# Interleaved token blocks and product streams from the last column to the first in a decoder layer, with two gaps of 128 bytes

## What is computed

```
h = rms_norm(x, attn_norm_g);  proj = h @ w_in                      # 2048 x 13312
kv = rms_norm(mem, mem_norm_g) @ w_mem_kv                           # 2048 x 2048
merged = (sigmoid(g_da) * (o_da @ w_o_da) + sigmoid(g_ret) * (o_ret @ w_o_ret)
          + sigmoid(g_mem) * (o_mem @ w_o_mem))
x = x + merged @ w_out
hf = rms_norm(x, ffn_norm_g)
x = x + (silu(hf @ w_ffn_gate) * (hf @ w_ffn_up)) @ w_ffn_down      # width 5632
```

## Time and profile before

| | us |
|---|---|
| median of 2 runs | 1623.02 (1622.66 to 1623.38) |
| span of the profiled execution | 1620.8 |
| PE busy | 1613.9 |
| DVE busy | 1305.7 |
| ACT busy | 915.7 |
| POOL busy | 80.6 |

### The profile page before, as it was taken

The page is one execution under the profiler, slowest core; times in us unless marked ns, Lnnn a source line. Parts: engine busy times, 40 slices in busy tenths (PEclk is TensorE's granted clock), DMA queues, the critical chain, the costliest instruction groups (busy, mean ns, idle before and its releaser), DMA issues.

```text
span 1620.8 us, 19825 instructions
## 1 busy us (share of the span) xinstructions
PE 1613.9 (100%) x7355; PEld 1336.1 (82%) x7355; DVE 1305.7 (81%) x1361; ACT 915.7 (56%) x993; POOL 80.6 (5%) x73
## 2 busy tenths in 40 slices
PE   9999999999999999999999999999999999999999
PEld 7888888888888888888888888888888888888887
DVE  5565658898677777787975589999999999999995
ACT  6654555555555544444554455665656655656653
POOL 0000000000011000000000000100100100100101
PEclk9999999999999999999999999999999999999999
DMA  9776555666645555566666746868868868868866
GB/s 351 268 214 194 157 150 177 213 201 196 193 156 168 165 162 172 180 186 202 206 233 192 258 147 210 256 211 254 243 216 245 252 206 251 246 217 240 251 213 177
DMA packets 178013, 341.45 MB, mean 211 GB/s; under 512 B 11792, under 2 KB 16400, under 8 KB 177168
## 3 DMA queue, kind: packets, MB, share of 16 engines
q1 hardware_dynamic: 167056, 319.45, 60.8%
q0 software_dynamic: 10880, 20.97, 7.1%
HBM read 317.31 MB, written 2.10 MB: 197 GB/s over the span
## 4 chain that ended last, share of the span: by engine, by line
PE 85%; issue 11%; DVE 1%; POOL 1%; DMA 1%; ACT 0%; DVEq 0%; ACTq 0%; SPq 0%; POOLq 0%
PE acc L1600 38%; PE at L1692 9%; PE at L1691 9%; PE at L1690 9%; PE acc L1692 5%; PE acc L1690 5%; PE acc L1691 5%; PE at L1600 3%; PE at L1622 2%; POOL rstd L487 1%; PE at L1653 0%; PE at L1670 0%; DMA raw<-in_w_mem_kv 0%; DMA raw<-in_w_in 0%; DVE w_lo L938 0%
## 5 line engine op out<-in xcount | busy, mean ns | idle before, releaser
L938 DVE TENSOR_TENSOR w_lo<-raw,w_hi 128x1024 fp32r<-128x1024 f32 x313 | 378.9, 1223 | 196.0 <-ACT w_hi L514 190.7
L514 ACT ACTIVATE w_hi<-raw 128x1024 fp32r<-128x1024 f32 x313 | 330.6, 1060 | 341.9 <-PE acc L1600 274.0
L1600 PE MATMUL acc<-w_hi,hT_hi 128*128 128x512 f32 x664 | 262.8, 396 | 0.0
L1600 PE MATMUL acc<-w_hi,hT_lo 128*128 128x512 f32 x664 | 258.8, 390 | 0.0
L1600 PE MATMUL acc<-w_lo,hT_hi 128*128 128x512 f32 x664 | 258.6, 390 | 0.0
L866 ACT ACTIVATE f_hi<-sum 128x2048 fp32r<-128x2048 f32 x60 | 115.3, 1922 | 122.0 <-DVE sum L1479 118.8
L1600 PE MATMUL acc<-w_hi,oT_hi 128*128 128x512 f32 x384 | 151.2, 394 | 1.1 <-DVE oT_lo L964 1.1
L1600 PE MATMUL acc<-w_hi,oT_lo 128*128 128x512 f32 x384 | 149.7, 390 | 0.0
L1600 PE MATMUL acc<-w_lo,oT_hi 128*128 128x512 f32 x384 | 149.4, 389 | 0.0
L1445 DVE TENSOR_TENSOR f_raw_rest<-f_raw,f_hi 128x2048 fp32r<-128x2048 f32 x64 | 145.3, 2284 | 4.3 <-ACT f_hi L856 4.3
L1600 PEld LDWEIGHTS acc<-w_hi,hT_hi 128*128 128x128 f32 x664 | 124.7, 188 | 27.4 <-issue 1.3
(11 more groups left out here) (348 smaller groups left out, 2858.6 us busy)
## 6 DMA issues: line engine op xcount, KB each, us to landing
raw<-in_w_in SPq DMA_DIRECT2D x208, 512.0 KB, 3.8
f_raw<-in_w_ffn_down SPq DMA_DIRECT2D x88, 512.0 KB, 5.0
f_raw<-in_w_ffn_gate SPq DMA_DIRECT2D x80, 512.0 KB, 4.0
f_raw<-in_w_ffn_up SPq DMA_DIRECT2D x80, 512.0 KB, 5.2
proj<-down POOLq DMA_DIRECT2D x40, 512.0 KB, 6.5
raw<-in_w_mem_kv SPq DMA_DIRECT2D x32, 512.0 KB, 5.7
raw<-in_w_out SPq DMA_DIRECT2D x32, 512.0 KB, 3.9
raw<-in_w_o_mem SPq DMA_DIRECT2D x16, 512.0 KB, 5.0
```

Of the source, the lines that this page charges most:

```text
L514: act.activation(w_hi[:, s % RING], raw[:, s % RING], ACT.Copy).then_inc(hi_done, 1)
L938: v.tensor_tensor(w_lo[:, s % RING], raw[:, s % RING], w_hi[:, s % RING].bitcast(F32), ALU.subtract).then_inc(lo_done, 1)
L1600: e = pe.matmul(dst, a[:, k0 + k, tok], w[:, s % RING, k, :], start=first and k == 0 and n == 0, stop=last and k == 1 and n == 2)
```

## The change

Three things, with the same number of instructions on each engine.

- The tokens of the two blocks are interleaved in `hT`, `aT` and the `cmb` tiles: token block `t` is now every second word (`t::TB`), and the four combinations lie as two interleaved pairs. The transposes that fill `hT` and `aT` write every second word of PSUM, and the host lays out the transposed input in that order. `oT` stays as it was.
- Each product of 512 columns streams its moving operand from the last column to the first, and writes its output in that order too, so that the result is the same.
- A tile of 32 unused words (128 bytes) stands behind `hT_hi` and another behind `hT_lo`.

```diff
@@ -135,7 +135,9 @@
         sb("align", [P, ALIGN])
         hT_hi = sb("hT_hi", [P, KD, TOK], F32R)
+        sb("gap_hi", [P, 32])
         hT_lo = sb("hT_lo", [P, KD, TOK], F32R)
+        sb("gap_lo", [P, 32])
...
-            ("rows_t1", rows_tile, F32), ("sum1", quad_tile, F32), ("cmb_hi", [P, 4, 4, P], F32R),
+            ("rows_t1", rows_tile, F32), ("sum1", quad_tile, F32), ("cmb_hi", [P, 4, 2, P, 2], F32R),
...
@@ -1426,17 +1428,16 @@
-                a11, a12 = pairs[:, :, 0, 0:P], pairs[:, :, 1, 0:P]
-                a21, a22 = pairs[:, :, 0, P:2 * P], pairs[:, :, 1, P:2 * P]
-                v.tensor_tensor(mixed[:, :, 3], a11, a21, ALU.subtract).then_inc(done, 1)
-                step(v.tensor_tensor(mixed[:, :, 0], a22, a21, ALU.subtract), done, 3)
...
+                a11, a12, a21, a22 = (pairs[:, :, k, t::TB] for t in range(TB) for k in range(2))
+                v.tensor_tensor(mixed[:, :, 1, :, 1], a11, a21, ALU.subtract).then_inc(done, 1)
+                step(v.tensor_tensor(mixed[:, :, 0, :, 0], a22, a21, ALU.subtract), done, 3)
...
             def three_passes(s, hi, lo, k0, p, k, t, first, last):
-                tok = slice(t * P, (t + 1) * P)
+                tok = slice(t, TOK, TB) if hi is hT_hi else slice(t * P, (t + 1) * P)
                 dst = acc[p][:, t, :] if p < 2 else at[:, 2 * p - 4 + t, :]
                 for n, (a, w) in enumerate(((hi, w_hi), (hi, w_lo), (lo, w_hi))):
-                    e = pe.matmul(dst, a[:, k0 + k, tok], w[:, s % RING, k, :],
+                    e = pe.matmul(dst[:, ::-1], a[:, k0 + k, tok], w[:, s % RING, k, ::-1],
                                   start=first and k == 0 and n == 0, stop=last and k == 1 and n == 2)
...
-                        e = turn(at[:, k % 4, t * P:(t + 1) * P], src[:, t, c0 + k * P:c0 + (k + 1) * P])
+                        e = turn(at[:, k % 4, t:TOK:TB], src[:, t, c0 + k * P:c0 + (k + 1) * P])
...
             def product(dst, hi, lo, whi, wlo, first, last):
 
+                dst, whi, wlo = dst[:, ::-1], whi[:, ::-1], wlo[:, ::-1]
                 pe.matmul(dst, hi, whi, start=first, stop=False)
...
             def block_a(t, k):
-                return hT_hi[:, k, t * P:(t + 1) * P], hT_lo[:, k, t * P:(t + 1) * P]
+                return hT_hi[:, k, t::TB], hT_lo[:, k, t::TB]
...
             def turn_acts(dst):
                 for k in range(4):
                     for t in range(TB):
-                        c0 = (k % 2) * 256 + t * P
-                        e = turn(dst[:, k // 2, c0:c0 + P], gt[:, t, k * P:(k + 1) * P])
+                        c0 = (k % 2) * TOK
+                        e = turn(dst[:, k // 2, c0 + t:c0 + TOK:TB], gt[:, t, k * P:(k + 1) * P])
...
             def combined(i, c):
-                return cmb_hi[:, i, c, :] if i < 4 else cmb_hi4[:, i - 4, c, :], cmb_lo[:, i, c, :]
+                hi = cmb_hi[:, i] if i < 4 else cmb_hi4[:, i - 4]
+                return hi[:, c // 2, :, c % 2], cmb_lo[:, i, c // 2, :, c % 2]
...
-        "x_t": inputs["x"][0].T, "mem_t": inputs["mem"][0].T,
+        "x_t": inputs["x"][0].T.reshape(D, TB, P).transpose(0, 2, 1).reshape(D, TOK), "mem_t": inputs["mem"][0].T,
```

More of the change, by code:

```diff
@@ L163, in program @@
                     for t in range(TB):
-                        for name, shape, dt in (("r_cmb", [P, 4, 4, P], F32R), ("r_sum", [P, 4, NCOL], F32R if stage else F32),
+                        for name, shape, dt in (("r_cmb", [P, 4, 2, P, 2], F32R), ("r_sum", [P, 4, NCOL], F32R if stage else F32),
                                                 ("r_hi", [P, 4, NCOL], F32R), ("r_act", [P, 2 * NCOL], F32)):
@@ L168, in program @@
                 for name, shape, dt in (("r_rows", [P, 4, 4, P], F32), ("r_whole", [P, 2, TOK], F32),
-                                        ("r_mixed", [P, 4, P], F32)):
+                                        ("r_mixed", [P, 2, P, 2], F32)):
                     branch[0, name, 0] = overlay.enter_context(nc.sbuf_tensor(name, shape, dt))
@@ L834, in _ @@
                     act.wait_ge(cmb_f, 5)
-                    act.activation(cmb_hi[:], sums[1][:].rearrange("p q (c m) -> p q c m", c=4),
+                    act.activation(cmb_hi[:], sums[1][:].rearrange("p q (a m b) -> p q a m b", a=2, b=2),
                                    ACT.Copy).then_inc(cmb_split, 1)
@@ L838, in _ @@
                     act.wait_ge(cmb_f4, 5)
-                    act.activation(cmb_hi4[:], sums[0][:, 2:4].rearrange("p q (c m) -> p q c m", c=4),
+                    act.activation(cmb_hi4[:], sums[0][:, 2:4].rearrange("p q (a m b) -> p q a m b", a=2, b=2),
                                    ACT.Copy).then_inc(cmb_split, 1)
@@ L1069, in memory_attention @@
                 if i is not None:
[L1070 to L1073, removed]
+                    a11, a12, a21, a22 = (p_whole[:, k, t::TB] for t in range(TB) for k in range(2))
+                    v.tensor_tensor(p_mixed[:, 1, :, 1], a11, a21, ALU.subtract).then_inc(p_cmb, 1)
+                    step(v.tensor_tensor(p_mixed[:, 0, :, 0], a22, a21, ALU.subtract), p_cmb, i * 5 + 3)
+                    step(v.scalar_tensor_tensor(out=p_mixed[:, 0, :, 1], in0=p_mixed[:, 0, :, 0], scalar=-1.0, in1=a11,
                                                 op0=ALU.mult, op1=ALU.subtract), p_cmb, i * 5 + 4)
-                    v.tensor_tensor(p_mixed[:, 2], a12, p_mixed[:, 1], ALU.add).then_inc(p_cmb, 1)
+                    v.tensor_tensor(p_mixed[:, 1, :, 0], a12, p_mixed[:, 0, :, 1], ALU.add).then_inc(p_cmb, 1)
                 i = head_slot(x, 6)
@@ L1315, in _ @@
                     if s == 2:
[L1316 to L1319, removed]
+                        a11, a12, a21, a22 = (r_whole[:, k, t::TB] for t in range(TB) for k in range(2))
+                        v.tensor_tensor(r_mixed[:, 1, :, 1], a11, a21, ALU.subtract).then_inc(r_cmb, 1)
+                        step(v.tensor_tensor(r_mixed[:, 0, :, 0], a22, a21, ALU.subtract), r_cmb, i * 5 + 3)
+                        step(v.scalar_tensor_tensor(out=r_mixed[:, 0, :, 1], in0=r_mixed[:, 0, :, 0], scalar=-1.0, in1=a11,
                                                     op0=ALU.mult, op1=ALU.subtract), r_cmb, i * 5 + 4)
-                        v.tensor_tensor(r_mixed[:, 2], a12, r_mixed[:, 1], ALU.add).then_inc(r_cmb, 1)
+                        v.tensor_tensor(r_mixed[:, 1, :, 0], a12, r_mixed[:, 0, :, 1], ALU.add).then_inc(r_cmb, 1)
                     if s == 6:
@@ L1428, in combine @@
                                      hT_lo[:, 2 * q0:2 * q1, :].bitcast(F32), ALU.add), done, 1)
-                a11, a12 = pairs[:, :, 0, 0:P], pairs[:, :, 1, 0:P]
-                a21, a22 = pairs[:, :, 0, P:2 * P], pairs[:, :, 1, P:2 * P]
-                v.tensor_tensor(mixed[:, :, 3], a11, a21, ALU.subtract).then_inc(done, 1)
-                step(v.tensor_tensor(mixed[:, :, 0], a22, a21, ALU.subtract), done, 3)
-                step(v.scalar_tensor_tensor(out=mixed[:, :, 1], in0=mixed[:, :, 0], scalar=-1.0, in1=a11, op0=ALU.mult,
+                a11, a12, a21, a22 = (pairs[:, :, k, t::TB] for t in range(TB) for k in range(2))
+                v.tensor_tensor(mixed[:, :, 1, :, 1], a11, a21, ALU.subtract).then_inc(done, 1)
+                step(v.tensor_tensor(mixed[:, :, 0, :, 0], a22, a21, ALU.subtract), done, 3)
+                step(v.scalar_tensor_tensor(out=mixed[:, :, 0, :, 1], in0=mixed[:, :, 0, :, 0], scalar=-1.0, in1=a11, op0=ALU.mult,
                                             op1=ALU.subtract), done, 4)
-                step(v.tensor_tensor(mixed[:, :, 2], a12, mixed[:, :, 1], ALU.add), done, 5)
-            mixed4 = sums[1][:].rearrange("p q (c m) -> p q c m", c=4)
+                step(v.tensor_tensor(mixed[:, :, 1, :, 0], a12, mixed[:, :, 0, :, 1], ALU.add), done, 5)
+            mixed4 = sums[1][:].rearrange("p q (a m b) -> p q a m b", a=2, b=2)
             last = sums[0][:, 0:2].rearrange("p q (k c) -> p q k c", k=2)
-            mixed1 = sums[0][:, 2:4].rearrange("p q (c m) -> p q c m", c=4)
+            mixed1 = sums[0][:, 2:4].rearrange("p q (a m b) -> p q a m b", a=2, b=2)
             def low_whole(f, p, u):
@@ L1717, in combined @@
                 def combined(c):
-                    return p_cmb_hi[:, i, c, :], p_cmb_lo[:, i, c, :]
+                    return p_cmb_hi[:, i, c // 2, :, c % 2], p_cmb_lo[:, i, c // 2, :, c % 2]
                 pe.wait_ge(lo_done, g + 2)
@@ L1847, in combined @@
                 def combined(c):
-                    return r_cmb_hi[:, i, c, :], r_cmb_lo[:, i, c, :]
+                    return r_cmb_hi[:, i, c // 2, :, c % 2], r_cmb_lo[:, i, c // 2, :, c % 2]
                 pe.wait_ge(lo_done, g + 2)
@@ L1960, in down_half @@
                 for k in range(4):
-                    e = product(at[:, 2 * (n % 2) + t, :], hi[:, k, t * P:(t + 1) * P],
-                                lo[:, k, t * P:(t + 1) * P], *whole(f, p, u, k), k == 0, k == 3)
```

(2 more changed lines are left out.)

8 lines of the change are left out of this document (4 added, 4 removed).

## The result

The changed kernel takes 1663.78 us (two runs, 1663.71 and 1663.84) against 1623.02: slower by the ratio 1.0251, 95% interval 1.0207 to 1.0295. The forecast was 1561 us, faster, with a range of 1550 to 1638; the time lies above it. The profiled execution's span is 1661.9 us, 41.1 more than before.

The account below looks back on a forecast made before the run. TensorE's start-to-start interval, 6771 x 0.2268 us, was taken to bound 95% of the span. Gains of 30.8 (products without oT), 7.6 (oT) and 24.1 us (feed-forward loop) sum to 62.5, giving 1561 us, range 1550 to 1638.

Parts of the forecast that it names:

- The excess: 512-column products start each 0.2268 us, 11.3 ns over the 0.2155 of plain float32 rows; 76.5 us over 6771 products.
- the loop's second bound: Feed-forward loop: VectorE's chain, 59.7 us a round, outlasts TensorE's 59.1, so the loop gives 24.1 us and not 30.5.
- the sum: Whole kernel: 30.8 + 7.6 + 24.1 = 62.5 us gained, taking the profiled span from 1620.8 to 1558.3 us.
- the split: Feed-forward loop, splitting of the weights (lines 1445 to 1458): claimed late next, so TensorE would begin to wait for it.
- the 120 transposes: Transposes writing every second word of the accumulator: no cost taken; 13 us if spaced writes halved their rate.
- VectorE's stepped operations: Forming the cmb operands with a step of two words: nothing on the path; even twice their time is 14 us.
- The change, part by part: 512-column products: reversal, stepped weights and shifted offsets let stream and load run side by side; stepped products reach 0.2155 us.
- plain products: Float32 products of 256 columns, 0.2155 us each: said to carry the same weight load and pay no excess.
- the doubled excess: Upper bound for the new interval of 512-column products, priced as a rival: 11.3 ns more each on 5427 products.
- half of the excess: The 1344 oT products, reversed only: 5.65 ns gained each, 7.6 us, bounds 0 and 15.2.
- (b): Rival on 5427 stepped-weight products: loads touching twice the memory double the excess, 61 us, 1684 us, slower; chance 0.17.
- Rival (a): 512-column products: nothing meets, the excess is a data-type fee; 1623 to 1636 us; chance 0.22 with its smaller-gain variant.

Follow-up runs that it names:

- e14: Kernel before, each 512-column stream reading its first word 512 times, weight loads unchanged: 0.2163 us from start to start.
- e1: Kernel before with only the reversal, every 512-column product streaming and writing from last column to first: 1664.31 us, ratio 1.0254.
- e3: Kernel before with only the read of the moving operand reversed, output written forward: 1663.41 us, one run.
- e4: Kernel before with only the output written from the last column, moving operand read forward: 1623.58 us, one run.
- e6: Changed kernel without reversal and without gaps, so the interleaving (step of two words) alone: 1657.14 us, ratio 1.0207.
- e5: Kernel before with only the two gaps of 128 bytes behind the halves of hT: 1636.11 us, ratio 1.0083.
- e13: Kernel before, each weight load of a 512-column product reading one word 128 times: 0.2317 us from start to start.
- e15: Kernel before with one-word weight loads, and stream and output from last column to first: 0.2333 us from start to start.
- e7: Kernel before with the second pass of each product cut to 64 of its 128 tokens: 1639.98 us.
- e12: Kernel before with gaps of 16 bytes behind each half of hT: 1639.49 us, ratio 1.0100.

## Why the prediction was wrong

**What held.** The bound, and the way to read it: TensorE's start-to-start distance times 6771 is 95% of the span, before and after. The excess is real, and the interval goes down to 0.216 us in e14, which doesn't compute the layer. And the loop's second bound: e14 gives the sum a test that the change didn't. Two of its rounds:

```profile
1117.66:1177.74 60.08, 59.81 (x279) 51.63 (x278) 58.55 (x45) 38.29 (x30) 4.75 (x4) 1.00 0.81 245
1177.74:1237.83 60.09, 59.81 (x279) 51.63 (x278) 58.56 (x45) 38.29 (x30) 4.75 (x4) 1.00 0.81 245
```

60.08 us, where the prediction had VectorE's chain at 59.7 and TensorE's at 59.1; e14's span is 1563.6 us where the sum said 1558.3. TensorE now waits for the split at L1458 (first line, whole span), and the wait of VectorE at L1485 shrinks from 24.1 us in ten rounds to 7.4 in nine (second line, 1000 to 1550 us):

```profile
PE at L1691 <- DVE sum_rest L1458: 2.6, 10, 0.3
DVE proj L1485 <- PE acc L1693: 7.4, 9, 0.8
```

Since 0.8 us a round are left of that wait, the round is not held by VectorE alone, as the prediction had it: a small miss. Also as costed: nothing for the 120 transposes and for VectorE's stepped operations.

**The step that failed** is the one headed "The change, part by part". From a correct pair of observations (the excess varies behind transposes; plain products with the same load don't pay) it concluded that the stream and the weight load meet, and from that that reversed direction, doubled step and new offsets would let them run side by side, which takes the 11.3 ns of excess off each product. Each of the three does the opposite: reversal alone adds 6.5 ns (e1), and it is the read that does it (e3, e4), the step alone 6.5 (e6), the offsets alone 4.3 (e5), the last two for products with the weights they touch. e13 shows that the load's walk isn't needed for the excess, and e15 that the reversed pace doesn't need it either. The prediction also gives no reason why a reversed stream should pass the load more easily; no row shows in which order a load reads its words. The argument had left out that the products that pay nothing also stream at half the pace: the thing that differed in the earlier trace rows was the stream, which the text says in its own words, and it then looked for the culprit in the load.

**Then the value.** Between the bounds for the new interval, 0.2155 and the doubled excess of 0.238 us, I took the lower end as the row nearest in kind. It was not: those rows have a forward stream in another type, and the case asked about had a reversed one. For a layout that no row shows there was no ground for either end, and nothing in the trace excluded a loss for the direction alone. The truth, 0.2333, is 58% of the way from the old interval to the upper bound. For the oT products I took half of the excess as a gain; they lost 6.5 ns.

**The rivals.** The one on the slow side, (b), had the right sign with 0.17 and a price of 1684 us, from the step of the weights. The step does cost (e6), by 6.5 ns and not by the 11.3 of (b), near the 6 from which (b) decides; but in the changed kernel it adds nothing, since products without it lose the same. So the cost that (b) names exists, but it isn't what made the changed kernel slower; that (b) had the sign right is luck. That the reversal alone could cost had no rival. Rival (a), a fee of the data type, is refuted in its premise by e14, where the type is the same and the fee is gone, and by the result.

**Where a page was drawn on.** The formula of the Trainium skill, "TensorE: Matmul & The Clock Gate", section "Back-to-back issue gap", which it gives for an isolated matmul and which comes to 215.8 ns for 512 columns, is approached by e14 alone, which reads one word (216.3 on the mean). The rows of 256 columns agree with it only when a plain float32 column is counted as two steps, which the prediction took from its 0.84 ns a column. The sentence of "SBUF — State Buffer", section "Who interferes with whom", in the Trainium skill, that TensorE's two read ports are independent, doesn't agree with e5, e6 and e13: a change in the load or in its offset to the stream moved the interval of the stream by 4 to 7 ns. By the rule of "PSUM — Partial Sum Buffer", section "Specifications", on patterns that are not contiguous, again of the Trainium skill, reversed and stepped writes might have cost; e4 (0.2266 us) and the eight transposes in 1.04 us show no cost.

**What stays open** is why the forward stream has a good pace of 0.2268 us that a change in the load of any kind (length, step, place, one word) disturbs, while the reversed one stood at 0.2333 under each load that it was tried with. Between 100 and 140 us every interval of the kernel before is 226 or 227 ns; those of e5 run from 226 to 235, those of e7 from 224 to 236. The first is a regular pattern that is lost, as it is behind the transposes; its cause isn't shown. A load read from its last word, and a stream with no load under it, weren't tried. That a version below 0.2268 us exists for a stream that does walk is not shown; nothing tried came near it, and no version here that computes the layer beats the kernel before.

## What to carry to other kernels

Where TensorE never waits, measure start to start: a few ns there, times thousands of products, are the whole difference. As far as this kernel shows, read float32r streams upward through memory, keep their weights contiguous and all tiles on the grid they had, and change one of these at a time, since the losses cover each other and don't add. An excess over a floor shows that something costs, not what: before forecasting that it goes away, name the row that shows it gone under the layout in question.

## What the runs showed of the hardware that was not expected

- A 512-column float32r stream read from its last column takes 6.5 ns more (0.2333 for 0.2268 us), in blocks of 16 bytes too; an output written from the last column takes nothing more.
- The same stream reading one word takes 0.2163 us: about 10.5 ns of the 226.8 go when the moving operand doesn't walk.
- Less to load made it slower: 64 weights for 128 in every third product shortened that load from 188 to 134 ns and raised the mean interval by 3 ns; loads of one word raised it by 4.9.
- Shifts of hT by as little as 16 and 32 bytes against the streamed tiles cost 4.3 ns for a product with weights from hT, 1% of the kernel (e12).
